# Gated delta rule in chunks of 64: block-diagonal chunk matrices, kept whole or as their blocks

## The chip, the core and the metric

The kernel runs on one core of a Trainium2 chip. TensorE (PE in the profile) multiplies, VectorE (DVE), ScalarE (ACT) and GpSimd (POOL) work on the elements, SyncE (SP) issues the DMA transfers. The metric is the device time of one execution in microseconds (us); lower is better. All data are fp32.

## The reference, cut to what matters

The program is two models in a row: two layers of a hybrid transformer block, then a second block whose token mixer is a gated delta rule, run forward and backward in time, followed by a mixture of 16 experts. The change touches the delta rule only: 4 heads of width 128, two directions, a context of 256 tokens (states alone, no queries) and then 512 tokens with queries, in chunks of 64.

```python
idx = jnp.arange(CHUNK)                                   # CHUNK = 64
incl = idx[:, None] >= idx[None, :]
decay = jnp.where(incl, jnp.exp(jnp.minimum(g[..., :, None] - g[..., None, :], 0.0)), 0.0)
m = jnp.where(idx[:, None] > idx[None, :], jnp.einsum('bhnik,bhnjk->bhnij', k_beta, kc) * decay, 0.0)
p = -m
t_inv = eye + p
for _ in range(CHUNK.bit_length() - 2):                   # five times
    p = p @ p
    t_inv = t_inv @ (eye + p)
w_blk = jnp.einsum('bhnij,bhnjk->bhnik', t_inv, k_beta * jnp.exp(g)[..., None])
u_blk = jnp.einsum('bhnij,bhnjv->bhniv', t_inv, vc * bc)
def advance(s, w_n, u_n, kt_n, sd_n):                     # once per chunk, in order
    u_new = u_n - jnp.einsum('bhik,bhkv->bhiv', w_n, s)
    return s * sd_n + jnp.einsum('bhik,bhiv->bhkv', kt_n, u_new), u_new
# with queries: o_n = q_dec @ s + (q k^T * decay) @ u_new
```

## The kernel before

Each engine has a program of its own, written out by hand in order, and the engines meet at counting semaphores. In the delta stage the class `Delta` (lines 499 to 522) counts named events: `says("KK", ins)` marks an instruction as the event KK of its engine, `needs("dve", "LT")` waits for an event of another. The order of each engine's list is the order of its code: PE lines 1189 to 1280, ACT 1736 to 1760, POOL 1885 to 1931, DVE 2298 to 2364.

The stage runs NT = 6 steps. A step takes a tile of 128 tokens (two chunks of 64) for each direction, and 4 heads for each direction, which are 8 units (U8; the first four are "f", the last four "b"). Steps 0 and 1 are context (no queries), steps 2 to 5 have queries (`x` is true). Each unit's chunk matrix is stored as 128 by 128 with two diagonal blocks of 64 by 64 that matter; the masks `tri` and `strict` make the rest zero. `pair(i)` is a pair of PSUM banks that holds 8 such matrices; there are four pairs.

The parts of a step, by event:
- Head. DVE TRILA (line 2315) spreads the log decays; PE G (1218) sums them with a matrix of ones, and KK, QK (1222, 1224) multiply keys by keys and keys by queries; PE KTOK and VTOK (1226, 1230) turn keys and values. DVE SUB and MIN (2319, 2321) and ACT E, EG (1746, 1748) make the decay matrix and the decay of the queries. POOL ETS and ETI (1903) mask it. DVE LT and QKD (2324, 2328) multiply it into KK and QK. PE L turns the result, DVE PM (2330) scales it by minus beta, PE PT turns it back, ACT PT (1754) copies that out.
- Rounds. Five doubling rounds on PE (1239 to 1253): SQ squares p, SQT squares its transpose (four rounds), TT multiplies it into the inverse; each for f and then b. ACT copies SQ out (1758), DVE copies SQT and adds TT (2337, 2340). Through the helper `each` (1206) all run as one matmul of 128 by 128 per unit.
- Tail. PE WT and U (1256, 1257), then for each of the two chunks WS, with queries Y (1273), and SU; at the end, with queries, X (1280). DVE U0f and so on (2350) subtract, S0f and so on (2355) update the state ST8, Y0 and X0 and so on (2362, 2364) add to the output. POOL scales keys, values and states (1914).

A matmul of the code is two passes through the array in the trace (fp32), each with its weight load; a transpose is one.

After the stage come a head norm, the output projection, the router, and the experts (PE line 1362), whose weights SP loads (line 716) once PE has signalled that the output projection is over (line 1305).

Of the kernel before, what the change touches and what calls it, by code (L numbers as in the profile page):

```python
# [99 lines left out]
K_TRI, K_STRICT = N_FIRST, N_FIRST + 2 * P  # L100
K_SAME = K_STRICT + 2 * P
# [7 lines left out]
def shape_constants():  # L109
# [9 lines left out]
    before = i[:, None] <= i[None, :]  # L119
    for d, m in enumerate((before, before.T)):  # L120
        c[:, K_TRI + d * P:K_TRI + (d + 1) * P] = m & same
        c[:, K_STRICT + d * P:K_STRICT + (d + 1) * P] = m & same & (i[:, None] != i[None, :])
# [27 lines left out]
def build(nc, A, out, debug=None):  # L150
    with ExitStack() as ctx:
# [192 lines left out]
        tri = c2[:, 0:2 * P].rearrange("p (d n) -> p d n", d=2)  # L344
        strict = c2[:, K_STRICT - K_TRI:K_STRICT - K_TRI + 2 * P].rearrange("p (d n) -> p d n", d=2)
# [20 lines left out]
        tail_half = take(NT * U8, 2)  # L366
# [26 lines left out]
        PTA, PTB, TT, ST8 = [view(i * U8 * P, U8, P, of=zf) for i in range(4)]  # L393
# [40 lines left out]
        def pair(i):  # L434

            return banks[:, 2 * i:2 * i + 2, :].rearrange("p b (h n) -> p (b h) n", n=P)

# [46 lines left out]
        def events(step):  # L484
# [3 lines left out]
                "pe": ["G", "KK"] + x * ["QK"] + ["KTOK", "VTOK", "L", "PT"]  # L488
# [3 lines left out]
                "dve": ["TRILA", "SUB", "MIN", "LT"] + x * ["QKD"] + ["PM", "TT0"]  # L492
                + [f"{n}{r}{d}" for r in r5 for n in (("SQT", "TT") if r < 5 else ("TT",)) for d in "fb"]
                + ["U"] + [f"{n}{c}{d}" for c in (0, 1) for n in ("U", "S") for d in "fb"] + x * ["Y0", "X0", "Y1", "X1"],
                "act": ["E"] + x * ["EG"] + ["KTOK", "VTOK", "PT"] + [f"SQ{r}{d}" for r in r5 for d in "fb"] + ["WT"],
                "pool": ["ETS", "ETI"] + x * ["QD"] + ["KBG", "KT0", "KT1", "VB", "SD0", "SD1"],
# [228 lines left out]
        def _(pe):  # L725
# [447 lines left out]
            for d in range(2):  # L1173
                pe.matmul(gs[:, :, d * DH:(d + 1) * DH], tri[:, d, :], la[:, :, d * DH:(d + 1) * DH], start=True, stop=True)
# [14 lines left out]
            for step in range(NT):  # L1189
# [16 lines left out]
                def each(i, lhsT, rhs, turn=False, units=slice(0, U8)):  # L1206
                    for un in range(U8)[units]:
                        o = pair(i)[:, un, :]
                        mm = pe.transpose(o, lhsT(un), ident) if turn else \
                            pe.matmul(o, lhsT(un), rhs(un), start=True, stop=True)  # L1210
                    return mm


                needs("dve", "TRILA")
                if step == 0:
                    pe.wait_ge(l2_ok, 2 * DH)
                for d in range(2):
                    mm = pe.matmul(ps[d][:, :], ones, E[:, d * DH:(d + 1) * DH, :].rearrange("p u n -> p (u n)"),
                                   start=True, stop=True)
                says("G", mm)  # L1220
                key = lambda un: kT[:, un % DH, cols(un)]
                says("KK", each(1, key, key))
                if x:
                    says("QK", each(2, key, lambda un: qT[:, un % DH, xcols(un)]))

                says("KTOK", each(3, key, None, True))
                needs("dve", "SUB")
                if x:
                    needs("act", "EG")
                says("VTOK", each(0, lambda un: vT[:, un % DH, cols(un)], None, True))  # L1230

                needs("dve", "LT")
                says("L", each(1, lambda un: ETS[:, un, :], None, True))
                needs("dve", "PM")
                says("PT", each(2, lambda un: PA[:, un, :], None, True))
# [3 lines left out]
                for r in range(1, 6):  # L1239
                    p0, pt0, p1 = Ps[(r - 1) % 2], PTs[(r - 1) % 2], Ps[r % 2]  # L1240
                    for d, units in DIRS.items():
                        if r == 1:
                            needs("act", "VTOK")
                        else:
                            needs("dve", f"SQT{r - 1}{d}")
                        says(f"SQ{r}{d}", each(3, lambda un: pt0[:, un, :], lambda un: p0[:, un, :], units=units))
                    if r < 5:
                        for d, units in DIRS.items():
                            says(f"SQT{r}{d}", each(0, lambda un: p0[:, un, :], lambda un: pt0[:, un, :], units=units))
                    for d, units in DIRS.items():  # L1250
                        needs("act", f"SQ{r}{d}")
                        needs("dve", f"TT{r - 1}{d}" if r > 1 else "TT0")
                        says(f"TT{r}{d}", each(1 if r % 2 else 2, lambda un: p1[:, un, :], lambda un: TT[:, un, :], units=units))
                needs("dve", "TT5b")
                needs("pool", "VB")
                says("WT", each(3, lambda un: KBG[:, un, :], lambda un: TT[:, un, :]))
                says("U", each(0, lambda un: TT[:, un, :], lambda un: VB[:, un, :]))
                needs("act", "WT")

                for c in range(2):  # L1260
                    for d, units in DIRS.items():
# [6 lines left out]
                        says(f"WS{c}{d}", each(1, lambda un: PTB[:, un, :], lambda un: ST8[:, un, :], units=units))  # L1268
                    if x:
                        for un in range(U8):  # L1270
                            h = c if un < DH else 1 - c
                            part = slice(h * CHUNK, (h + 1) * CHUNK)
                            mm = pe.matmul(pair(3)[:, un, part], ST8[:, un, :], EG[:, un, part], start=True, stop=True)
                        says(f"Y{c}", mm)
# [1199 lines left out]
```

## Time and profile before

| what | value |
|---|---|
| median of 3 runs | 3387.52 us (3384.53 to 3387.95) |
| the profiled execution, its own time | 3385.13 us |
| its span in the profile | 3382.6 us |
| PE busy / DVE / ACT / POOL | 86% / 35% / 22% / 7% of the span |
| delta stage in the trace | 2261 us to 2636.4 us: 375 us, 11% of the span |
| granted TensorE clock, mean | 0.94 |

The profile gives for each engine when each instruction began and how long it took, and what ended the idle time before it. PE is the matmul side of TensorE, PEld its weight loads. The chain is the path of work that ended last, followed back from the end: what is on it sets the time. PEclk is the share of full clock that was granted: 1.00 is 2.4 GHz, and a value between 0.5 and 1 is a mixture of that and 1.2 GHz over the stretch.

### The profile page before, as it was taken

Reading aid. Unit: us, or ns where it says so; the run is one execution under the profiler, and the core shown is the slowest. Engines: PE = TensorE matmul, PEld = TensorE weight load, DVE = VectorE, ACT = ScalarE, POOL = GpSimd, SP = SyncE. Lnnn points to the kernel's source line nnn. Section 1 sums busy time; section 2 is a strip of 40 time slices with the busy share of each in tenths; the row PEclk is TensorE's granted clock in tenths of the full one; section 3 lists DMA queues with packets and bytes.
Section 4 is the critical chain, followed back from the end, with each engine's and each line's share of the span. In section 5 each row is a group of like instructions: output and inputs, shape, how many; then the busy total and the mean of one; then the engine's idle time right before and its main releaser. Section 6 shows DMA issues by size and latency. Waiting matters only on the chain.

```text
span 3382.6 us, 31088 instructions
## 1 busy us (share of the span) xinstructions
PE 2896.7 (86%) x11890; PEld 1825.1 (54%) x11890; DVE 1170.3 (35%) x1663; ACT 751.2 (22%) x1169; POOL 241.1 (7%) x156
## 2 busy tenths in 40 slices
PE   7978888899989798788999959978888758777778
PEld 3324566688854235565888834648788444222223
DVE  0176234433330392544333334364444340000001
ACT  2133232322221242332212131141111022000001
POOL 0120000000000300000000006012332010000000
PEclk9989999999999899999999989889989869999999
DMA  4123211224230132211333231000000026999990
GB/s 143 50 75 120 80 50 57 68 81 113 84 113 22 50 136 88 75 50 50 87 94 100 81 109 44 32 25 1 1 1 1 0 87 275 410 409 410 409 381 25
DMA packets 256104, 379.57 MB, mean 112 GB/s; under 512 B 9153, under 2 KB 170078, under 8 KB 255838
## 3 DMA queue, kind: packets, MB, share of 16 engines
q1 hardware_dynamic: 255966, 377.72, 31.3%
q8 instruction: 88, 1.44, 0.2%
q14 instruction: 50, 0.41, 0.0%
HBM read 375.59 MB, written 2.10 MB: 112 GB/s over the span
## 4 chain that ended last, share of the span: by engine, by line
PE 66%; DMA 13%; DVE 12%; ACT 4%; issue 3%; POOL 1%; SPq 0%; DVEq 0%; ACTq 0%; POOLq 0%; PEldq 0%
PE banks L790 29%; PE banks L766 11%; PE banks L1093 9%; DMA ring<-in_w_up 8%; PE banks L1210 7%; DMA arena<-in_w_down 4%; DVE arena L2080 4%; PE banks L1362 2%; PE banks L776 1%; PE banks L782 1%; PE banks L1025 1%; PE banks L1340 1%; DVE stat L2061 1%; PE banks L1111 1%; DVE arena L2261 1%
## 5 line engine op out<-in xcount | busy, mean ns | idle before, releaser
L1549 ACT ACTIVATE w_hi<-ring 128x2048 fp32r<-128x2048 f32 (+1 forms) x100 | 174.4, 1746 | 544.2 <-PE banks L790 544.2
L790 PE MATMUL banks<-ffn_x_hi,w_hi 128*128 128x512 f32 x704 | 277.7, 394 | 16.7 <-DVE ffn_x_lo L1999 16.6
L790 PE MATMUL banks<-ffn_x_lo,w_hi 128*128 128x512 f32 x704 | 275.6, 391 | 0.0
L790 PE MATMUL banks<-ffn_x_hi,w_lo 128*128 128x512 f32 x704 | 275.4, 391 | 0.0
L1985 DVE TENSOR_TENSOR w_lo<-ring,w_hi 128x2048 fp32r<-128x2048 f32 (+1 forms) x100 | 207.5, 2077 | 78.8 <-ACT w_hi L1549 77.4
L1362 PE MATMUL banks<-ring,std 128*64 128x512 f32 x640 | 153.6, 603 | 46.3 <-DMA ring<-in_w_up 26.5
L766 PE MATMUL banks<-xT,ring 128*128 128x512 f32 (+1 forms) x416 | 183.5, 604 | 1.2 <-ACT taps L1453 1.2
L2080 DVE SCALAR_TENSOR_TENSOR arena<-arena,taps 128x512 f32<-128x512 f32 x240 | 163.3, 743 | 0.0
L790 PEld LDWEIGHTS banks<-ffn_x_hi,w_hi 128*128 128x128 f32 x704 | 132.9, 189 | 51.5 <-issue 17.9
L2449 DVE TENSOR_TENSOR gates<-gates,banks 128x512 f32<-128x512 f32 x16 | 11.0, 688 | 423.9 <-PE banks L1362 423.9
L1093 PE MATMUL banks<-zT,ring 128*128 128x512 f32 x320 | 144.7, 610 | 7.7 <-issue 6.9
L790 PEld LDWEIGHTS banks<-ffn_x_hi,w_lo 128*128 128x128 f32 x704 | 133.2, 189 | 28.0
L790 PEld LDWEIGHTS banks<-ffn_x_lo,w_hi 128*128 128x128 f32 x704 | 133.3, 189 | 26.6
L1210 PE MATMUL banks<-zT,arena 128*128 128x128 f32 x1152 | 141.9, 281 | 5.2 <-DVE zT L2340 4.7
L1210 PEld LDWEIGHTS banks<-zT,arena 128*128 128x128 f32 x1152 | 136.4, 197 | 6.9 <-DVE zT L2340 5.8
L790 PE MATMUL banks<-ffn_hidden_hi,w_hi 128*128 128x512 f32 x352 | 136.9, 389 | 0.0
L790 PE MATMUL banks<-ffn_hidden_lo,w_hi 128*128 128x512 f32 x352 | 136.9, 389 | 0.0
L790 PE MATMUL banks<-ffn_hidden_hi,w_lo 128*128 128x512 f32 x352 | 136.9, 389 | 0.0
L766 PEld LDWEIGHTS banks<-xT,ring 128*128 128x128 f32 (+1 forms) x416 | 79.7, 192 | 104.1 <-issue 104.1
L2182 DVE TENSOR_TENSOR squares<-gates,banks 128x512 f32<-128x512 f32 x44 | 30.2, 687 | 293.6 <-PE banks L790 293.6
L1362 PEld LDWEIGHTS banks<-ring,std 128*64 128x64 f32 x640 | 40.1, 136 | 158.7 <-DMA ring<-in_w_up 64.4
L766 PE MATMUL banks<-arena,ring 128*128 128x256 f32 (+2 forms) x384 | 115.7, 463 | 9.6 <-DVE arena L2036 9.6
(363 smaller groups left out, 4493.6 us busy)
## 6 DMA issues: line engine op xcount, KB each, us to landing
ring<-in_w_up SPq DMA_DIRECT2D x48, 1024.0 KB, 18.4
arena<-in_w_down SPq DMA_DIRECT2D x48, 1024.0 KB, 18.4
ring<-in_ffn_w_in SPq DMA_DIRECT2D x88, 512.0 KB, 4.5
ring<-in_w_gate SPq DMA_DIRECT2D x32, 1024.0 KB, 18.0
ring<-in_w_mod SPq DMA_DIRECT2D x24, 1024.0 KB, 7.2
ring<-in_xa_w_kv SPq DMA_DIRECT2D x16, 1024.0 KB, 6.2
zT<-in_w_gate SPq DMA_DIRECT2D x16, 1024.0 KB, 18.5
zT<-in_w_up SPq DMA_DIRECT2D x16, 1024.0 KB, 18.4
```

Source lines behind the costliest of these rows:

```text
L766: mm = pe.matmul(bank[0:m, 0:width], weights(k), rhs(k), start=(k == 0), stop=(k == n - 1))
L776: mm = pe.matmul(ps[bank][:, :], ones, zT[:, t, :], start=(t == 0), stop=(t == KT - 1))
L782: mm = pe.matmul(ps[bank + 1][:, :], ones, squares[:, t % 2, :], start=(t == 0), stop=(t == KT - 1))
L790: mm = pe.matmul(bank[:, :], weights(wp, k), rhs(rp, k), start=(k == 0 and wp == rp), stop=(k == n - 1 and wp == 1))
L1025: mm = pe.matmul(ps[4 + v][:, :], xv[:, kt, h * XD + v * P:h * XD + (v + 1) * P], probsT[:, kt, :], start=(kt == 0), stop=(kt == MT - 1))
L1093: mm = pe.matmul(out, weights(k), rhs(k), start=(k == 0), stop=(k == n - 1))
L1111: mm = pe.matmul(ps[1 + m % 2][:, 0:n], ones, squares[:, t % 2, 0:n], start=(t == 0), stop=(t == KT - 1))
L1210: pe.matmul(o, lhsT(un), rhs(un), start=True, stop=True)
L1362: mm = pe.matmul(bank[n * CAP:(n + 1) * CAP, :], tokens, weights[:, n * 512:(n + 1) * 512], start=first, stop=last)
L1549: nc.scalar.activation(w_split[n % 2][0][:, 0:m], raw[n % 2][:, 0:m], ACT.Copy).then_inc(f_hi.sem, 1)
L1985: V.tensor_tensor(lo[:, 0:m], raw[n % 2][:, 0:m], hi[:, 0:m].bitcast(F32), ALU.subtract).then_inc(f_lo.sem, 1)
L2080: V.scalar_tensor_tensor(out=acc, in0=x, scalar=c, in1=acc, op0=ALU.mult, op1=ALU.add)\
```

## The change

The chunk matrices keep only their diagonal blocks: a unit's matrix becomes 128 rows by 64 columns (rows 0 to 63 hold the first chunk's block, rows 64 to 127 the second's), so tiles of 8 x 128 columns become 8 x 64. The helper `small` multiplies each unit in two matmuls of 64 by 64 by 64, one on the array's upper left quarter and one on its lower right. Masks are applied by DVE as KKM and QKM straight from PSUM; POOL's ETS and ETI go, and POOL makes the product QKD. The decay of the queries gets matmuls of its own (GX) into pair 3, where KTOK comes next and waits for EG. The keys' tail scaling needs one POOL product (KT) where it took two (KT0, KT1), since SU reads only the rows of its chunk. KK and QK move ahead of G, and wait for the last step's last addition (X1 or S1b). L and PT become products with a block of the identity. WT, U, SU and X contract over 64 rows, WS has 64 columns of weights. The small set-up step `tail_half` goes.

```diff
-        E, ETS, ETI, EG, KBG, KT0, KT1, VB, PA, PB = [take(U8, P) for _ in range(10)]
+        E, GD, ETS, ETI, PA, PB, PTA, PTB, TT = [take(U8, CHUNK) for _ in range(9)]
+        KBG, KD, VB = [take(U8, P) for _ in range(3)]
+        EG = take(2, U8, CHUNK)
+        def blocks(i):
+            return banks[:, 2 * i:2 * i + 2, 0:DH * CHUNK].rearrange("p b (h n) -> p b h n", n=CHUNK)
+        def by_chunk(i):
+            return banks[:, 2 * i:2 * i + 2, :].rearrange("p c (u n) -> p c u n", n=CHUNK)
...
-                needs("dve", "TRILA")
-                for d in range(2):
-                    mm = pe.matmul(ps[d][:, :], ones, E[:, d * DH:(d + 1) * DH, :].rearrange("p u n -> p (u n)"),
-                                   start=True, stop=True)
-                says("G", mm)
-                key = lambda un: kT[:, un % DH, cols(un)]
-                says("KK", each(1, key, key))
+                def small(i, lhsT, rhs, units=slice(0, U8)):
+                    for un in range(U8)[units]:
+                        for c, rows in enumerate(CHUNKS):
+                            mm = pe.matmul(blocks(i)[rows, un // DH, un % DH, :], lhsT(un, rows), rhs(un, rows),
+                                           start=True, stop=True)
+                    return mm
+                if step == 0:
+                    pe.wait_ge(l2_ok, 2 * DH)
+                else:
+                    needs("dve", "X1" if step - 1 >= CTX // P else "S1b", step - 1)
+                says("KK", small(1, key, key))
+                if x:
+                    says("QK", small(2, key, lambda un, rows: qT[:, un % DH, xtokens(un, rows)]))
+                needs("dve", "TRILA")
+                for d in range(2):
+                    for rows in CHUNKS:
+                        mm = pe.matmul(blocks(0)[rows, d], ones[rows, 0:CHUNK], E[rows, d * DH:(d + 1) * DH, :],
+                                       start=True, stop=True)
+                says("G", mm)
+                if x:
+                    for c, rows in enumerate(CHUNKS):
+                        mm = pe.matmul(by_chunk(3)[:, c], ones[rows, :], E[rows, :, :], start=True, stop=True)
+                    says("GX", mm)
+                    needs("act", "EG")
+                says("KTOK", transposed(3, lambda un: kT[:, un % DH, cols(un)]))
...
-                        says(f"SQ{r}{d}", each(3, lambda un: pt0[:, un, :], lambda un: p0[:, un, :], units=units))
+                        says(f"SQ{r}{d}", small(3, lambda un, rows: pt0[rows, un, :], lambda un, rows: p0[rows, un, :], units))
...
-                says("WT", each(3, lambda un: KBG[:, un, :], lambda un: TT[:, un, :]))
-                says("U", each(0, lambda un: TT[:, un, :], lambda un: VB[:, un, :]))
+                        mm = pe.matmul(by_chunk(3)[:, c, un, :], KBG[rows, un, :], TT[rows, un, :], start=True, stop=True)
+                        mm = pe.matmul(pair(0)[rows, un, :], TT[rows, un, :], VB[rows, un, :], start=True, stop=True)
...
+                            mm = pe.matmul(pair(1)[CHUNKS[half_no], un, :], WT[:, half_no, un, :], ST8[:, un, :],
+                                           start=True, stop=True)
+                            mm = pe.matmul(pair(2)[:, un, :], KD[rows, un, :], VN[rows, un, :], start=True, stop=True)
+                            mm = pe.matmul(by_chunk(1)[:, c, un, :], VN[rows, un, :], ETI[rows, un, :], start=True, stop=True)
...
-                for name, dst, m in (("ETS", ETS, strict), ("ETI", ETI, tri)):
-                    for d in range(2):
-                        ins = G.tensor_tensor(dst[:, r, :], E[:, r, :], masked(m)[d], ALU.mult)
+                    says("QKD", G.tensor_tensor(ETI, ETI, E, ALU.mult))
-                says("KT0", scaled(KT0, KT1, th[:, :, 0]))
-                says("KT1", scaled(KT1, KT1, th[:, :, 1]))
+                says("KT", scaled(KD, KD, tail[:, step, :]))
...
-                    ins = V.tensor_tensor(E[:, r, :], tri[:, d:d + 1, :].broadcast_to([P, DH, P]),
-                                          la[:, step, r].unsqueeze(2).broadcast_to([P, DH, P]), ALU.mult)
-                says("TRILA", ins)
+                says("TRILA", V.tensor_tensor(by_dir(E), each_dir(tri), each_col(la[:, step, :]), ALU.mult))
+                says("KKM", V.tensor_tensor(by_dir(ETS), blocks(1), each_dir(strict), ALU.mult))
+                    says("QKM", V.tensor_tensor(by_dir(ETI), blocks(2), each_dir(tri), ALU.mult))
+                says("SUB", V.tensor_tensor(by_dir(GD), blocks(0), each_col(gsum[:, step, :]), ALU.subtract))
+                says("LT", V.tensor_tensor(ETS, ETS, E, ALU.mult))
```

## Rows read from the trace of the kernel before


**Rows 1.** The page: span, and granted clock in 40 equal slices of it.
```profile
span 3382.6 us, 31088 instructions
...
PEclk9989999999999899999999989889989869999999
```

**Rows 2.** Windows by step: length; busy PE, PEld, DVE, ACT, POOL; PEclk, DMA, GB/s.
```profile
2261.00:2317.00 56.00, 47.82 (x372) 45.10 (x372) 25.21 (x33) 10.98 (x16) 17.16 (x10) 0.91 0.00 1
2317.00:2374.00 57.00, 48.19 (x372) 45.47 (x372) 26.41 (x35) 10.90 (x15) 17.16 (x10) 0.91 0.00 1
2374.00:2439.50 65.50, 55.40 (x436) 52.00 (x436) 30.12 (x40) 11.94 (x16) 19.51 (x12) 0.92 0.00 1
2439.50:2506.10 66.60, 56.53 (x436) 53.41 (x436) 30.09 (x40) 11.94 (x16) 19.51 (x12) 0.90 0.00 1
2506.10:2571.20 65.10, 55.73 (x436) 53.05 (x436) 31.07 (x41) 11.93 (x16) 19.51 (x12) 0.92 0.00 1
2571.20:2636.40 65.20, 55.64 (x436) 52.64 (x436) 30.84 (x39) 11.94 (x16) 19.51 (x12) 0.92 0.00 1
```

**Rows 3.** The chain through step 3: start, length, what.
```profile
2439.45 1.21 DVE arena L2315 x2
...
2440.71 3.38 PE banks L1218 x4
...
2447.24 4.98 POOL arena L1903 x4
...
2456.73 1.03 ACT zT L1754
...
2457.81 28.30 PE banks L1210 x224
...
2486.13 0.70 DVE zT L2340
...
2486.87 5.62 PE banks L1210 x48
2492.49 1.73 PE banks L1273 x16
```

**Rows 4.** The chain through step 1, context only.
```profile
2333.05 27.57 PE banks L1210 x224
...
2361.39 3.85 PE banks L1210 x32
```

**Rows 5.** Timeline inside the rounds: start, length, instruction, idle before and releaser.
```profile
2471.57 1.95 PE L1210 MATMUL banks<-arena,zT 128*128 128x128 f32 x16
2472.67 0.60 ACT L1758 ACTIVATE arena<-banks 128x512 f32<-128x512 f32 x1 [3.87 <-PE banks L1210]
2473.36 3.74 PE L1210 MATMUL banks<-zT,arena 128*128 128x128 f32 x32
```

**Rows 6.** Timelines: a 128-column stream, then the experts' 64-column one and its loads.
```profile
2097.09 7.03 PE L1093 MATMUL banks<-zT,ring 128*128 128x512 f32 x16
...
2902.41 1.94 PE L1362 MATMUL banks<-ring,std 128*64 128x512 f32 x8 [0.62 <-DMA ring<-in_w_gate]
...
2902.41 0.20 PEld L1362 LDWEIGHTS banks<-ring,std 128*64 128x64 f32 x4 [1.50 <-DMA ring<-in_w_gate]
```

**Rows 7.** Two weight loads by line: ns least, median, most.
```profile
L1362 PEld LDWEIGHTS banks<-ring,std x640: 132/137/137, 2817.6 to 3285.0; 128*64 128x64 f32 x160
...
L1210 PEld LDWEIGHTS banks<-zT,arena x1152: 186/192/333, 2279.8 to 2631.4; 128*128 128x128 f32 x192
```

**Rows 8.** A window of the expert stage (columns as in Rows 2, clock third from the end).
```profile
2900.00:3000.00 100.00, 76.55 (x326) 21.04 (x326) 3.16 (x6) 8.42 (x13) 0.00 (x0) 1.00 1.03 409
```

**Rows 9.** Groups by form: count, busy us, mean ns, idle before.
```profile
L2265 DVE TENSOR_TENSOR arena<-arena 128x256 f32<-128x256 f32 x4 | 1.7, 419 | 0.0
...
L1668 ACT ACTIVATE arena<-banks 128x256 f32<-128x256 f32 x8 | 3.1, 385 | 68.9 <-PE banks L1093 68.9
```

**Rows 10.** Waits of SP's own queue.
```profile
SPq L716 <- PEq L1305: 518.2, 1, 518.2
```

More of the change, by code:

```diff
@@ L118, in shape_constants @@
         c[NOPE + j, K_SWAP + NOPE + h + j] = 1.0
[L119 to L122, printed above, removed]
+    row, col = i[:, None] % CHUNK, i[None, :CHUNK]
+    for d, m in enumerate((row <= col, row >= col)):
+        c[:, K_TRI + d * CHUNK:K_TRI + (d + 1) * CHUNK] = m
+        c[:, K_STRICT + d * CHUNK:K_STRICT + (d + 1) * CHUNK] = m & (row != col)
+    c[:, K_EYE:K_EYE + CHUNK] = row == col
     c[:, K_SAME:K_SAME + P] = same
@@ L1204, in xcols, with transposed @@
                     return slice(t * P, (t + 1) * P)
-                def each(i, lhsT, rhs, turn=False, units=slice(0, U8)):
+                def transposed(i, src):
+                    for un in range(U8):
+                        mm = pe.transpose(pair(i)[:, un, :], src(un), ident)
+                    return mm
+                def small(i, lhsT, rhs, units=slice(0, U8)):
                     for un in range(U8)[units]:
-                        o = pair(i)[:, un, :]
-                        mm = pe.transpose(o, lhsT(un), ident) if turn else \
-                            pe.matmul(o, lhsT(un), rhs(un), start=True, stop=True)
-                    return mm
@@ L1234, in _ @@
+                says("L", small(1, lambda un, rows: ETS[rows, un, :], same_block))
                 needs("dve", "PM")
-                says("PT", each(2, lambda un: PA[:, un, :], None, True))
+                says("PT", small(2, lambda un, rows: PA[rows, un, :], same_block))
                 needs("act", "PT")
@@ L1753, in _ @@
                 needs("pe", "PT")
-                says("PT", A1(PTA, pair(2), ACT.Copy))
+                says("PT", A1(by_dir(PTA), blocks(2), ACT.Copy))
                 for r in range(1, 6):
@@ L2317, in _ @@
-                says("TRILA", ins)
-                needs("pe", "G")
-                says("SUB", V.tensor_tensor(E, pair(0), every(gsum[:, step, :]), ALU.subtract))
-                needs("dve", "SUB")
-                says("MIN", V.tensor_scalar(E, E, 0.0, None, ALU.min))
+                if step and step - 1 >= CTX // P:
+                    needs("pool", "QKD", step - 1)
+                says("TRILA", V.tensor_tensor(by_dir(E), each_dir(tri), each_col(la[:, step, :]), ALU.mult))
                 needs("pe", "KK")
-                needs("pool", "ETS")
@@ L2329, in _ @@
+                needs("dve", "SUB")
+                says("MIN", V.tensor_scalar(GD, GD, 0.0, None, ALU.min))
+                needs("act", "E")
+                needs("dve", "KKM")
+                says("LT", V.tensor_tensor(ETS, ETS, E, ALU.mult))
                 needs("pe", "L")
-                says("PM", V.tensor_tensor(PA, pair(1), every(nbeta[:, step, :]), ALU.mult))
+                says("PM", V.tensor_tensor(by_dir(PA), blocks(1), each_col(nbeta[:, step, :]), ALU.mult))
                 needs("act", "PT")
-                says("TT0", V.tensor_tensor(TT, PTA, ident.unsqueeze(1).broadcast_to([P, U8, P]), ALU.add))
+                says("TT0", V.tensor_tensor(TT, PTA, eye.unsqueeze(1).broadcast_to([P, U8, CHUNK]), ALU.add))
```

152 lines of the change are left out of this document (83 added, 69 removed).

## The prediction

> **What bounds the kernel now.** I read the page first for the span and the clock [rows 1], then windows for the time of each step of the delta stage [rows 2], then the chain through a step with queries [rows 3] and through one without [rows 4], and last the timeline inside the doubling rounds [rows 5]. The six steps take 56.0, 57.0, 65.5, 66.6, 65.1 and 65.2 us, 375.4 in all, one behind the other [rows 2]. In step 3 the chain has three stretches: a head of 18.4 us (2439.45 to 2457.81), in which each engine waits for another and POOL's masking alone takes 4.98; rounds of 29.1 (to 2486.87), in which PE is the chain for 28.3; and a tail of 19.3, mostly PE again [rows 3]. So PE's passes in the rounds and the hand-overs in the head are what a change can shorten. Behind the stage nothing catches up: SP's queue stands at the expert weights for 518.2 us until PE reports the output projection [rows 10], so the DMA-fed experts start earlier by whatever the delta stage gives up. I take it one for one.
>
> **The unit of the sum: a pass.** A group of 4 units, 8 passes with weights of 128 columns, takes 0.895 us: 16 passes start at 2471.57 and the next ones at 2473.36, and ACT starts on the first half 1.10 after its first pass, 0.20 behind its last slot [rows 5]. So a pass costs 0.112 and a hand-over 0.20 (0.05 from ACT or DVE to PE, as from 2439.45 + 1.21 to 2440.71 in [rows 3]). Halving the moving columns alone brings nothing: line 1273 moves 64 columns with weights of 128, and its 16 passes take 1.73, 0.108 each [rows 3]. What holds it is the weight load. Loads last 192 ns for 128 columns and 137 for 64 [rows 7], 55 ns for each 64 columns, so a pass of 64 by 64 should hold its part of the array for about 0.055 to 0.058. I take 0.058, a load in the same proportion above its 0.055 as 0.112 above the 0.108.
>
> The change needs twice the passes (two quarters per unit), so all hangs on whether quarters overlap. The experts' 64-column matmuls go to two halves of the array in turn: 8 passes of 512 columns take 1.94, while 16 such passes with 128 columns take 7.03 [rows 6]. Taken off the last pass's tail (about 0.2), that is 0.43 for two passes against 0.43 for one: they overlap fully, in fp32. Four loads of 0.14 lie within 0.20 there [rows 6], so the fourth starts at most 0.06 behind the first, and the array takes loads for both halves within one slot. I therefore price a pair of quarters at 0.058, 0.029 for a pass. No row shows two *row* parts overlapping; the bounds are full overlap and none, and I take overlap since the halves are the nearest row.
>
> **Head with queries**, from the last addition of the step before: KK 16 pairs, 0.05 to 0.98; QK to 1.91; G, 8 passes of 256 columns in 4 pairs of 0.215 (half of 0.43), to 2.77, with TRILA (0.69) long done; a change of tile shape, which I bound by nothing and one hand-over, at 0.2; GX, 4 passes of 512 in 2 pairs, to 3.83; hand-over; EG on ACT (1.03 for 1024 columns, as the copy in [rows 3]) to 5.06. That is a new wait: KTOK stands behind EG on PE, and VTOK, L and the rest behind KTOK. KTOK and VTOK, 16 single passes, end at 6.9. Beside them: DVE's KKM, QKM, SUB and MIN (0.70 each for 512 columns) end before 5, E on ACT (0.60 [rows 5]) follows EG to 5.7, LT ends at 6.4, so it is hidden. L with a shape change 7.1 to 8.03; PM to 8.93; PT to 9.90; ACT's copy to 10.7; the rounds start at 10.8. That is 7.6 less than 18.4. POOL's QD, QKD, KBG, KT and VB, some 10 us, lie under the rounds.
>
> **Head without queries**: no QK, GX or EG. G ends at 1.84, SUB, MIN (0.69 as the bound), E and LT end at 4.85 and are now what ends last, since VTOK is over at 3.8. Rounds start at 8.6 against 16.3 in step 1 (window start 2316.7 to 2333.05 [rows 2, 4]): 7.7 less.
>
> **Rounds.** A group of 4 units is 8 pairs, 0.464. In rounds 1 to 4 PE has six groups, 2.78. Is something else late? DVE takes 0.42 for 256 columns and ACT 0.39 [rows 9]: an SQT starts at 0.93, is copied by 2.02, needed at 2.78; DVE works 1.7 of 2.78. So PE stays the bound: 11.1. Round 5 is latency: SQ 0.46, hand-over, ACT 0.39, then TT, 2.0 in all; then DVE 0.42 with its hand-overs, 0.7. Sum 13.8, against 29.1 in step 3 and 28.3 in step 1 (2333.05 to 2361.39): 15.3 and 14.5 less.
>
> **Tail.** WT, U and X have twice the passes, but 128 columns of weights or of moving data keep each at 0.112, so as pairs they cost what they did (32 passes in pairs, 1.8). WS, Y and SU have as many passes as before and go group by group. DVE's and ACT's pieces there keep their sizes. I add 0.7 a step for three or four unhidden shape changes, and 1.0 for passes at the lower clock: the steps have a clock of 0.90 to 0.92 [rows 2] with head gaps above 1 us, and such gaps remain. Both are bounded below by nothing; above, 1.7 could be 4.
>
> **Sum.** Step 3 gains 7.6 + 15.3 - 1.7 = 21.2; the mean of the four steps with queries is 65.6 against 66.6, because of clock I no longer expect, so 20.2, times 4 is 80.8. Steps 0 and 1 gain 7.7 + 14.5 - 1.7 less 0.5 (mean 56.5 against 57.0) = 20.0 each, 40.0. The set-up step and the four small matmuls that replace two cancel within 0.5. The profiled execution took 3385.1, so 3385.1 - 120.8 = 3264.3; the median of the runs lies 2.4 above it: **3267 us**.
>
> **Rivals.**
> - *No overlap of quarters* (the change doesn't do what it says; ends slower). The stage issues 3392 passes of the small kind (576 in a step with queries, 544 without) and 512 in WT, U and X. One by one they cost 3392 x 0.029 = 98 and 512 x 0.056 = 29 more, G and GX 9 more: 3403. It decides from 89% of the overlap lost. Against it: the halves in [rows 6]. For it: no row has two row parts. A milder form is a rule that two row parts may not write one PSUM bank at a time: both quarters of a `small` write one bank, as do those of U and G, while WT, X and GX write two. Then 98 + 11 + 5 are lost: 3381, within 0.2% of before. The Trainium skill states it ("TensorEngine Tiling (Array Packing)", Restrictions and Gotchas): different row tiles cannot access the same PSUM bank simultaneously. The trace only has two column halves in one bank, which overlap.
> - *Row parts overlap only where their columns differ too.* WT, X and GX go one by one: 320 x 0.056 + 3.4 = 21 more, 3288.
> - *The instruction stream.* Quarters want a load and a pass every 0.029. The densest long stream of the trace has one every 0.112 [rows 5]; only a burst of four loads [rows 6] is denser. If the queue runs dry, each 0.01 a pass costs 34 us; gain and loss meet at 0.063, and at 0.112 the time would be 3577. The Trainium skill ("TensorE: Matmul & The Clock Gate", Part 1) gives about 62 ns for each matmul when hardware decoding is off; by that figure, an estimate, the sum would be near 3382, no change. No run here shows which decoding is on.
> - *The clock.* If a stage of small tiles were held at 1.2 GHz, passes double: 98 for the small ones and 99 for the rest, 3464. Against it: half-width weights run at a clock of 1.00 [rows 8].
>
> **From cases to numbers.** The forecast (3240 to 3290): 0.62. Row parts in one column range not overlapping (3288): 0.12. A stream somewhat slower than 0.029, up to 0.053 (3290 to 3350): 0.08, and up to 3381: 0.03. Bank rule, or a pace near the 0.063 where gain and loss meet: 0.07. Slower: no overlap 0.03, pace over 0.063 0.03, clock 0.02. A measurement of this kernel tells about 0.2% (7 us) from no change. So faster 0.85, same 0.07, slower 0.08. The range's low end is a slot of 0.055 and PE running WS and SU of the two directions beside one another, since they now sit in different parts of the array (up to 0.9 x 4 a step, 21 us): 3240. Its high end takes in the rows case and a stream of 0.05: 3345.
>
> **What would show it.** After: rounds of some 14 us in each step; six groups in 2.8; PE starts two by two; a window of a step with queries of about 45 us and of one without about 37; POOL gone from the chain; ACT's EG in the chain ahead of KTOK. Wrong if the small passes start 0.05 or more apart without a wait, or if the clock row of the stage falls below 0.8. The same gain must appear as an earlier start of the expert stage, whose length stays.

## The result, and the profile of the kernel after

The kernel after takes 3263.2 us (median of 4 runs, 3260.07 to 3264.21), against 3387.52 before: the ratio is 0.963, with a 95% interval of 0.962 to 0.9648, so 124 us less. The forecast was 3267, with a range of 3240 to 3345. The profiled execution took 3262.29 us; its span is 3260.5.

The page of the kernel after, its span and the granted clock in 40 slices, which answer to [rows 1]:

```profile
span 3260.5 us, 35240 instructions
...
PEclk9989999999999989999999997998999869999999
```

The same windows as in [rows 2], one for each step of the delta stage (length; busy PE, PEld, DVE, ACT, POOL; granted clock, DMA share, GB/s):

```profile
2262.50:2297.60 35.10, 30.57 (x696) 28.12 (x696) 18.40 (x34) 7.91 (x15) 9.86 (x5) 1.00 0.01 3
2297.60:2332.70 35.10, 30.57 (x696) 28.12 (x696) 18.95 (x35) 7.91 (x15) 9.85 (x5) 1.00 0.01 3
2332.70:2376.70 44.00, 37.81 (x796) 34.61 (x796) 22.87 (x40) 8.93 (x16) 13.87 (x8) 0.99 0.01 2
2376.70:2422.00 45.30, 39.06 (x796) 35.86 (x796) 22.92 (x40) 8.93 (x16) 13.87 (x8) 0.95 0.01 3
2422.00:2468.40 46.40, 40.22 (x796) 36.45 (x796) 22.86 (x40) 8.93 (x16) 13.86 (x8) 0.94 0.01 2
2468.40:2513.90 45.50, 39.26 (x796) 36.06 (x796) 22.89 (x39) 8.93 (x16) 13.88 (x8) 0.95 0.01 2
```

The stage takes 251.4 us where it took 375.4, so 124.0 of the time saved is here, and the two spans differ by 122.1. Each step has nearly twice the passes (796 against 436) in two thirds of the time, and its clock is higher (0.94 to 1.00 against 0.90 to 0.92). Behind the stage nothing catches up: the last 480.5 us of both kernels are the same work at the same pace. The first row below is that window after, the second the same window before; POOL is idle in both and the DMA share is 0.84 in both:

```profile
2780.00:3260.50 480.50, 371.32 (x1460) 116.11 (x1460) 27.52 (x42) 51.31 (x81) 0.00 (x0) 0.99 0.84 337
```

```profile
2902.00:3382.50 480.50, 371.35 (x1460) 116.15 (x1460) 27.51 (x42) 51.37 (x81) 0.00 (x0) 0.99 0.84 337
```

The wait of SP's queue that was 518.2 us [rows 10] is now this one, in the list of waits (engine, line, what it waits for: us in all, times, longest):

```profile
SPq L747 <- PEq L1377: 393.8, 1, 393.8
```

It is 124.4 shorter, as much as the stage gave up. The chain through step 3 (start, length, what), where [rows 3] had POOL's masks and passes of line 1210; KK and QK are the first row, G and GX the next two, then EG on ACT:

```profile
2376.74 3.33 PE banks L1249 x64
2380.07 1.01 PE banks L1273 x8
2381.08 1.08 PE banks L1278 x4
...
2382.19 1.03 ACT arena L1819
...
2383.26 1.97 PE banks L1241 x16
2385.23 1.11 PE banks L1249 x32
...
2388.30 0.61 ACT arena L1827
...
2388.95 12.35 PE banks L1249 x416
...
2401.32 1.17 PE banks L1249 x32
...
2402.51 0.43 DVE arena L2395
...
2402.99 2.00 PE banks L1312 x32
2404.99 1.89 PE banks L1318 x32
2406.89 1.51 PE banks L1332 x16
2408.40 1.93 PE banks L1338 x16
```

The reader is to see three things. First, the rounds are 14.0 us (2388.95 to 2402.94), where they were 29.1: 416 passes in 12.35, 0.0297 each. Second, POOL is gone from the chain; KTOK and VTOK (line 1241) begin 0.04 behind EG. Third, the head is 12.2 us and no longer a chain of three engines' turns only: its largest piece is KK and QK, 64 passes in 3.33, or 0.052 each, nearly twice what a pass costs in the rounds.

The timeline inside the rounds, as in [rows 5] (idle time before, and what ended it, in brackets):

```profile
2392.02 0.42 DVE L2395 TENSOR_TENSOR arena<-arena,banks 128x256 f32<-128x256 f32 x1
2392.21 3.38 PE L1249 MATMUL banks<-arena 64*64 64x64 f32 x110
...
2392.48 0.85 ACT L1831 ACTIVATE arena<-banks 128x256 f32<-128x256 f32 x2 [1.95 <-PE banks L1249]
2393.42 0.89 DVE L2392 COPY arena<-banks 128x256 f32<-128x256 f32 x2 [0.98 <-PE banks L1249]
...
2394.35 0.89 DVE L2395 TENSOR_TENSOR arena<-arena,banks 128x256 f32<-128x256 f32 x2
2395.28 0.38 ACT L1831 ACTIVATE arena<-banks 128x256 f32<-128x256 f32 x1 [1.95 <-PE banks L1249]
```

A round lasts 2.80 us (ACT starts at 2392.48 and 2395.28); DVE works 1.78 of it, ACT 0.85, and PE has no gap. The single starts in the trace come in pairs: of the intervals between starts of the 3392 passes of line 1249, 1617 are 6 or 7 ns and 1398 are 51 or 52 ns. So two quarters start together, and the next two follow 0.052 behind. One thing said of the change needs setting right: KK and QK contract over all 128 rows (the trace has them as 128*64), so their two passes are column halves of the array; quarters are G, L, PT, U and the products of the rounds. The starts of KK and QK in step 2 come in pairs just as well.

### The profile page after: what moved, and what is told of

It reads as the page before. It is cut to its first block, busy times and chain, and to the rows that moved or that the text cites. A ratio compares the mean times of both kernels' runs of the same rounds, so it can differ in the third digit from the quotient of the medians.

```text
span 3260.5 us, 35240 instructions
## 1 busy us (share of the span) xinstructions
PE 2797.1 (86%) x13982; PEld 1725.3 (53%) x13982; DVE 1124.2 (34%) x1656; ACT 733.2 (22%) x1169; POOL 203.9 (6%) x130
## 4 chain that ended last, share of the span: by engine, by line
PE 66%; DMA 14%; DVE 12%; ACT 4%; issue 3%; POOL 1%; SPq 0%; DVEq 0%; ACTq 0%; POOLq 0%; PEldq 0%
PE banks L821 30%; PE banks L797 11%; PE banks L1124 9%; DMA ring<-in_w_up 8%; DMA arena<-in_w_down 5%; DVE arena L2145 4%; PE banks L1249 3%; PE banks L1434 2%; PE banks L807 1%; PE banks L813 1%; PE banks L1056 1%; PE banks L1412 1%; DVE stat L2126 1%; PE banks L1142 1%; DVE arena L2326 1%
## 5 line engine op out<-in xcount | busy, mean ns | idle before, releaser
L821 PE MATMUL banks<-ffn_x_hi,w_hi 128*128 128x512 f32 x704 | 277.7, 394 | 16.4 <-DVE ffn_x_lo L2064 16.3
L1249 PE MATMUL banks<-arena 64*64 64x64 f32 (+1 forms) x3008 | 95.9, 224 | 15.1 <-DVE arena L2419 8.5
L1124 PEld LDWEIGHTS banks<-zT,ring 128*128 128x128 f32 x320 | 62.1, 195 | 82.1 <-issue 81.5
```

The lines of the kernel that those rows point to most:

```text
L821: mm = pe.matmul(bank[:, :], weights(wp, k), rhs(rp, k), start=(k == 0 and wp == rp), stop=(k == n - 1 and wp == 1))
L1124: mm = pe.matmul(out, weights(k), rhs(k), start=(k == 0), stop=(k == n - 1))
L1249: mm = pe.matmul(blocks(i)[rows, un // DH, un % DH, :], lhsT(un, rows), rhs(un, rows), start=True, stop=True)
```

## The experiments

Theory A is the prediction's: a pass on a quarter is paced by its weight load, the two quarters overlap, PE is the bound of the rounds, and the heads gain by the moved masks. Its rivals: quarters don't need each other (B in the first run), the stream of instructions or the copies set the pace, the moved columns set it, and the gain in the head is from elsewhere. Each run is compared with 3263.2 us, the kernel after, or with 3387.5, the kernel before; a ratio is always to the kernel before, run again beside it (medians of 3385.3 to 3386.6). A difference below some 7 us is told as what it is, not as a finding.

**1. The same passes, quarter by quarter.** All passes of one quarter of a group go first (8 where a group is one direction, 16 where it is both), then all of the other:

```diff
-                    for un in range(U8)[units]:
-                        for c, rows in enumerate(CHUNKS):
+                    for c, rows in enumerate(CHUNKS):
+                        for un in range(U8)[units]:
```

> After's kernel, with one line order changed: a group issues all its passes for the upper left quarter first and then all for the lower right, 8 and 8, where they took turns. Same passes, same waits. Theory A (quarters overlap because the next instructions in TensorE's queue go to the other quarter; it looks past a few waiting ones only): each pass then costs about 0.058 us alone, so 3392 x 0.029 = 98 us more at most, some 70 to 98 us over after (3333 to 3361). Rival B (the queue reaches past 16 instructions, or overlap is not what made the rounds short): no change, 3263.

Measured: 3311.4 us (3310.14 to 3313.84), ratio 0.9778 [0.9762, 0.9795], 48 more than after. Two pieces of its chain in step 2 (L, then the rounds), and the windows of the rounds in steps 1 and 2:

```profile
2358.62 1.85 PE banks L1249 x32
...
2363.82 16.79 PE banks L1249 x448
```

```profile
2317.90:2337.10 19.20, 19.16 (x448) 18.99 (x448) 8.89 (x18) 3.84 (x10) 1.16 (x1) 0.85 0.01 3
2363.80:2380.60 16.80, 16.77 (x448) 16.60 (x448) 8.62 (x18) 3.84 (x10) 5.04 (x3) 1.00 0.01 4
```

Where 16 passes of one quarter precede 16 of the other, 32 passes take 1.85, and the single starts in the trace lie 58 or 59 ns apart: this is the price of an unpaired pass that the prediction took. Only where the quarter changes are there three pairs of starts 4 or 5 ns apart. The rounds, with 8 and 8, show the same three pairs at a change, each time: of 8 starts 3 come 4 to 6 ns behind another, which leaves 5 slots of 58 ns, and a pass costs 0.037 at a clock of 1.00 (16.79 / 448). Theory A had not foreseen this part of the overlap, so the run falls below its 3333 to 3361. In five of the six steps the rounds also take 19.2 to 19.4 at a clock of 0.83 to 0.85. So the gain does rest on the order of the quarters; the 48 us are of two kinds, the lost overlap (3.3 us in the rounds of each step and 0.7 for each of KK, QK, L and PT, some 35 in all) and the lower clock (some 2.5 in the rounds of five steps, some 12 in all).

**2. Two and two.** To see how far ahead a pass may begin, the quarters change after two passes:

```diff
+                    some = list(range(U8)[units])
+                    for two in (some[k:k + 2] for k in range(0, len(some), 2)):
                         for c, rows in enumerate(CHUNKS):
-                            mm = pe.matmul(...)
+                            for un in two:
+                                mm = pe.matmul(...)
```

> The kernel after, with the quarters taken in turn by two units instead of one: two passes on the upper left quarter, then two on the lower right. Theory A: passes may begin ahead of an earlier one that still waits for its own quarter, over a reach of a few passes (the runs of eight in q1_order still ran at 0.037 a pass at full clock), so two and two overlap fully: 3262 to 3268 us, rounds 13.5 to 14. Rival B: only the very next pass can begin beside the one that runs; then of each four passes one pair overlaps and the pace is 0.043 a pass, 3392 x 0.014 = 49 us more, near 3310.

Measured: 3265.5 us (3262.8 to 3268.97), ratio 0.9646 [0.963, 0.9662]. The rounds in step 2 and in step 1:

```profile
2347.00:2359.40 12.40, 12.39 (x416) 12.26 (x416) 7.61 (x17) 3.46 (x9) 6.23 (x4) 1.00 0.02 4
...
2307.10:2321.70 14.60, 14.60 (x416) 14.50 (x416) 8.92 (x17) 3.46 (x9) 3.91 (x2) 0.83 0.01 3
```

The first is what the kernel after has (12.35), so alternation needn't be strict: runs of two overlap fully, and longer runs overlap for three passes at each change of quarter. The second row is step 1, 2.2 us longer at a clock of 0.83; the other five steps have 12.39 or 12.40. Whether the order brings that about isn't shown: in experiment 8 the rounds of step 4, with strict alternation, take 14.66 at 0.82.

**3. Twice the stream.** Each small product issued twice, with nothing else changed:

```diff
+                        for n in (64, CHUNK):
-                        for c, rows in enumerate(CHUNKS):
+                            for c, rows in enumerate(CHUNKS):
```

> After's kernel, but each small matmul is issued twice into the same place (the pair first, then the pair again), so 3392 passes more. Theory A (PE is what bounds the rounds, and a pair of passes costs 0.058): 3392 x 0.029 = 98 more, 3361. Rival B (rounds are held by the hand-overs to ScalarE and VectorE, so that passes have slack): clearly less, under 50 more.

Measured: 3358.6 us (3356.11 to 3362.03), ratio 0.9915 [0.9898, 0.9931], 95 more than after for 3392 more passes: 0.028 each. The rounds:

```profile
2325.91 26.37 PE banks L1250 x896
```

Theory A's price holds (26.37 / 896 = 0.0294), also over a stream that lasts 26 us without a gap. This also answers the rival of the instruction stream: a load and a pass every 0.029 us is sustained, an instruction each 15 ns, and the queue does not run dry.

**4. Fewer columns moved.** The same, where the extra pass moves 16 columns (q3_thin) or 32 (q4_half) of the 64:

```diff
-                        for n in (64, CHUNK):
+                        for n in (16, CHUNK):
```

> As q2_twice, but the first of the two issues moves 16 columns instead of 64; weights are loaded in full (64 columns). Theory A (the weight load sets the 0.058 of a pair): as much as q2_twice, 3361. Rival B (the moving columns set it): a quarter of it, some 25 more, 3288.

> The kernel after, with each small product issued twice as in q2_twice, where the first of the two moves 32 of the 64 columns. Theory A: a pass of a quarter is paced by its weight load and not by the columns that it moves, so the time is that of q2_twice, 3358 us, and each five rounds take 26.4 us with the clock at 1.00. Rival B: the columns set the pace, then the rounds are shorter by a quarter, about 20 us, near 3325. Rival C: what kept the clock at 0.50 in four steps of q3_thin does it here too, then the rounds of those steps take 48 us and the time is above 3420.

With 32 columns: 3358.0 us (3356.73 to 3360.08), ratio 0.9921 [0.9905, 0.9938], the same as in 3. Every step's rounds take 26.37 at a clock of 1.00, one of them here:

```profile
2374.80:2401.20 26.40, 26.35 (x896) 26.21 (x896) 8.24 (x18) 3.84 (x10) 4.66 (x3) 1.00 0.02 4
```

So half the columns in half the passes change nothing: the load sets the pace. With 16 columns the runs lie between 3397.09 and 3484.3, median 3475.07, and no ratio is given, since the runs themselves differ by 87 us. Even the shortest is 39 above the run with 32 columns. The trace is of an execution of 3468.66 us. The windows of its rounds in steps 0, 2 and 3:

```profile
2276.30:2324.40 48.10, 48.05 (x896) 47.86 (x896) 8.35 (x18) 3.83 (x10) 0.63 (x1) 0.50 0.01 2
...
2406.90:2433.20 26.30, 26.30 (x896) 26.17 (x896) 8.16 (x18) 3.83 (x10) 4.60 (x3) 1.00 0.02 4
2473.40:2521.40 48.00, 48.00 (x896) 47.82 (x896) 8.80 (x18) 3.83 (x10) 3.37 (x2) 0.50 0.01 3
```

At a clock of 1.00 the rounds take 26.3, so there too the load sets the pace, as theory A said. But in four of six steps (0, 3, 4 and 5) the clock stays at 0.50 or 0.51, 1.2 GHz, through rounds in which PE has not one gap, and they take 47.7 to 48.1. Neither theory expected it. The run differs from the one with 32 columns in that number alone, so thin passes are what brings it about; four such steps are 86 of the 111 us by which this execution is above the run with 32 columns. Why the same stream is granted full clock in two steps and not in the others stays open. The prediction's rival of the clock is therefore real for thinner passes and does not touch the kernel's own, of 64 columns.

**5. The copies of the rounds twice.** ACT's copy of SQ and DVE's of SQT are made a second time, into a spare tile:

```diff
+                        A1(XA[:, r % 2][:, units, :], blocks(3)[:, "fb".index(d)], ACT.Copy)
                         says(f"SQ{r}{d}", A1((PA, PB)[r % 2][:, units, :], blocks(3)[:, "fb".index(d)], ACT.Copy))
...
+                            V.tensor_copy(XV[:, r % 2][:, units, :], blocks(0)[:, "fb".index(d)])
                             says(f"SQT{r}{d}", V.tensor_copy((PTA, PTB)[r % 2][:, units, :], blocks(0)[:, "fb".index(d)]))
```

> The kernel after, with each copy of SQ on ScalarE and of SQT on VectorE in the rounds done a second time into a spare tile first. Theory A: PE is the bound of the rounds and both engines have slack (VectorE 1.8 of 2.8 us, then 2.6 of 2.8), so only round 5, which is latency, shows it: 0.4 us a step and some slips, +2 to +8 us, 3266 to 3271. Rival B: the rounds hang on the copies: 8 more copies of 0.43 us on VectorE in each of six steps, +21 us, 3284.

Measured: 3265.0 us (3262.72 to 3267.73), ratio 0.9642 [0.9626, 0.9658]: 1.8 more, just under theory A's 2 to 8 and far from 21. The end of the rounds in step 2 is where it shows:

```profile
2346.11 11.91 PE banks L1250 x400
...
2358.43 0.28 ACT arena L1833
...
2358.75 1.26 PE banks L1250 x32
```

Only round 5 waits for ACT's second copy. From 2346.11 to the end of DVE's last addition at 2360.47 it is 14.36 against 14.0 in the kernel after, and six times 0.36 is 2.2. So PE alone bounds the rounds, with at least the 0.9 us of slack on DVE that the two extra copies of a round took up.

**6. The masks of the head, put back.** The kernel after, with its masks made by POOL as before, on the narrow tiles:

```diff
-                "dve": ["TRILA", "KKM"] + x * ["QKM"] + ["SUB", "MIN", "LT", "PM", "TT0"]
+                "dve": ["TRILA", "SUB", "MIN", "LT"] + x * ["QKD"] + ["PM", "TT0"]
...
+                for name, dst, m in (("ETS", ETS, strict), ("ETI", ETI, tri)):
+                    says(name, G.tensor_tensor(by_dir(dst), by_dir(E), each_dir(m), ALU.mult))
```

> After's kernel with the masks back on GpSimd (ETS and ETI made from the decay, at the new width of 64 columns), LT and QKD from PSUM on VectorE; all else is after's. Theory A (at half width GpSimd's masks cost little): L about 0.7 us later and PM 0.2 behind QKD with queries, LT 1.3 later without, so 4 x 0.9 + 2 x 1.3 = 6 more, 3269. Rival B (the mask order is worth as much as in the wide kernel): 15 more or over, 3278.

Measured: 3273.4 us (3272.14 to 3275.48), ratio 0.9668 [0.9653, 0.9682], 10 more. In the chain of a step with queries stand

```profile
2393.26 2.53 POOL arena L1971 x2
...
2395.88 0.69 DVE arena L2384
```

so the masks alone, half as wide, cost 2.53 on POOL, and it is part of the head again (13.1 us from KK to the rounds, against 12.2, the 0.9 that theory A gave a step). The rest of the 10 is mostly clock. The rounds of steps 0 and 1, 12.35 in the kernel after, take 14.00 and 14.53 here, 3.8 more for the same 416 passes, and this is step 1:

```profile
2312.60:2327.10 14.50, 14.50 (x416) 14.39 (x416) 7.94 (x17) 3.45 (x9) 2.94 (x2) 0.83 0.02 5
```

In the other four steps they are as in the kernel after. What is left of the 10 is the 6 that theory A gave; the 3.8 of clock it did not have.

**7. The masks of the head alone, on the kernel before.** DVE applies the masks to KK and QK as they leave PSUM, at the full width of 128, and POOL makes the product QKD; PE's passes stay as they are:

```diff
-                "pool": ["ETS", "ETI"] + x * ["QD"] + ["KBG", "KT0", "KT1", "VB", "SD0", "SD1"],
+                "pool": x * ["QKD", "QD"] + ["KBG", "KT0", "KT1", "VB", "SD0", "SD1"],
...
+                    ins = V.tensor_tensor(ETS[:, r, :], pair(1)[:, r, :], strict[:, d:d + 1, :].broadcast_to([P, DH, P]), ALU.mult)
+                says("KKM", ins)
```

> The kernel before with one part of the change alone: the masks go from GpSimd to VectorE (straight from PSUM, while ScalarE makes the decay), at full width, and GpSimd makes only the product QKD. Whole matrices, no quarters. Theory A (the order and GpSimd's masks are the smaller part of the gain, the width and the quarters the larger): from the end of MIN to PM 5.1 us in place of 7.3 with queries and 4.0 in place of 6.9 without, so 4 x 2.2 + 2 x 2.9 = 15 less than before, 3373. Rival B (GpSimd's 5 us on the chain are the head's whole gain): 25 to 35 less, 3353 to 3362.

Measured: 3363.0 us (3359.24 to 3365.05), ratio 0.9929 [0.9912, 0.9945], 24 less than before, between what the two theories gave. Its rounds in step 3, with the same 224 passes that took 28.30 in [rows 3]:

```profile
2443.30:2468.70 25.40, 25.34 (x224) 25.15 (x224) 14.69 (x19) 5.97 (x10) 10.32 (x6) 1.00 0.01 2
```

They are 2.9 shorter, at a clock of 1.00; in the kernel before the same stretch (2457.80 to 2486.10) has 0.89. This is the step with the largest difference. Over the six steps the 224 passes take 26.82, 27.57, 26.86, 28.30, 28.10 and 27.81 before, and 26.86, 25.35, 26.98, 25.35, 26.81 and 25.35 here: 8.8 less in all, and nothing in steps 0 and 2. The six heads, each from its step's start to its rounds, give 16.4 (from 103.0 to 86.6), near theory A's 15. So the gain is theory A's, and with it clock in the rounds that neither theory had.

**8. The order of the transposes.** In a step with queries VTOK, which doesn't use pair 3, goes ahead of KTOK, so that less waits for EG:

```diff
+                    says("VTOK", transposed(0, lambda un: vT[:, un % DH, cols(un)]))
                     needs("act", "EG")
                 says("KTOK", transposed(3, lambda un: kT[:, un % DH, cols(un)]))
```

> After's kernel, but in steps with queries PE turns the values (VTOK, which waits only for SUB) before the keys (KTOK, which waits for EG), so that only half of the turning stands behind the new wait. Theory A (in after's trace LT ends at 2385.11 and L starts at 2385.17, so LT was as late as the turning and is what comes next): within 1 us of 3263. Rival B (the wait for EG was the head's bound): 0.9 x 4 = 3.6 less, 3260.

Measured: 3261.3 us (3259.18 to 3262.46), ratio 0.963 [0.9617, 0.9643], 1.9 less, which can't be told from nothing. The medians alone can't choose between the two theories, which are 3.6 apart. The trace can: from KK to the rounds step 3 takes 12.16 against 12.21 in the kernel after. The transposes leave the chain, and LT takes their place.

```profile
2379.20 1.02 ACT arena L1822
2380.22 0.53 ACT arena L1824
...
2380.78 1.36 DVE arena L2385
```

**9. No idle stretch between the steps.** The head's largest piece is KK and QK at a low clock. Here PE is given work of the next step while DVE still adds the output: TRILA of the next step is made behind the last state update, the additions are ordered Y, Y, X, X, and PE's order is QK, G, GX, KK, each behind the one event that frees its bank:

```diff
-                "pe": ["KK"] + x * ["QK"] + ["G"] + x * ["GX"] + ["KTOK", "VTOK", "L", "PT"]
+                "pe": x * ["QK"] + ["G"] + x * ["GX"] + ["KK"] + ["KTOK", "VTOK", "L", "PT"]
...
-                + ["U"] + [f"{n}{c}{d}" for c in (0, 1) for n in ("VN", "S") for d in "fb"] + x * ["Y0", "X0", "Y1", "X1"],
+                + ["U"] + [f"{n}{c}{d}" for c in (0, 1) for n in ("VN", "S") for d in "fb"]
+                + (step < NT - 1) * ["NEXT"] + x * ["Y0", "Y1", "X0", "X1"],
```

> After's kernel with the head of a step pulled under the tail of the one before: TRILA of the next step right behind S1b, the additions in the order Y0, Y1, X0, X1, the Y ones before X has ended, and on PE QK, G, GX before KK, so that only KK waits for the last addition. Same instructions. Theory A (in steps behind one with queries PE stands idle for 2.8 us before KK and then runs KK and QK at half clock, 3.3 us in place of 2.1): L comes 4 to 6 us earlier in steps 3 to 5 and 1 to 2 in steps 1 and 2, in all 14 to 20 less, 3243 to 3249, and the clock of steps 3 to 5 goes from 0.95 to near 1. Rival B (VectorE's queue is the head's bound, the additions and six products in a row): under 8 less, 3255 or more.

Measured: 3243.6 us (3241.11 to 3243.85), ratio 0.9578 [0.9565, 0.9591]: 20 less than after, faster than both kernels. Its step 3 begins right behind X, the first row (chain, then the window of the step):

```profile
2371.32 1.73 PE banks L1360 x31
2373.05 1.08 PE banks L1250 x32
2374.13 1.01 PE banks L1276 x8
2375.14 1.06 PE banks L1283 x4
2376.20 1.08 PE banks L1250 x32
```

```profile
2373.00:2413.20 40.20, 37.90 (x799) 34.70 (x798) 22.15 (x40) 8.94 (x16) 13.88 (x8) 1.00 0.01 3
```

QK and KK take 1.08 each, 2.16 together against 3.33, and the step 40.2 us at a clock of 1.00 against 45.3 at 0.95. PE is busy for 37.9 of the 40.2. Of the 5.1 us, 2.8 are the idle time between the steps, 1.2 the clock of KK and QK, and 1.1 the wait for EG, which KK now covers. Step 1 doesn't gain as theory A had it: from the rounds of step 0 to its own it takes 36.5 us against 35.1, with G at 1.92 and KK at 1.82 at the lower clock.

## Why the prediction was right

**The pass and its overlap.** The pair of quarters was priced at 0.058, a pass at 0.029; the rounds give 0.0297, and the extra passes of experiment 3 cost 0.028. The load of 64 columns takes 135 ns in the trace, as the 137 of [rows 7]. The unpaired 0.058 stands in experiment 1, in the starts 58 or 59 ns apart. The choice of the column halves in [rows 6] as nearest row for row parts was right.

**Rounds.** 13.8 was said and 14.0 came in all six steps; six groups take 2.80 where 2.78 was said. DVE is not late, and experiment 5 bounds its slack.

**Head without queries.** 8.6 was said, and step 1 has 8.6 (2297.63 to 2306.22).

**Head with queries.** 10.8 was said; steps 2 to 5 have 11.0, 12.2, 13.4 and 12.4. This is the term that was mis-sized. KK and QK were priced at 1.86. They take 2.09 in step 2, where little idle time stands before them, and 3.33, 3.68 and 3.54 in steps 3 to 5, where PE has stood idle while DVE adds the outputs, for 2.84 us in step 3, and the first passes behind that run at the lower clock. This is the window of the first 2.76 us of KK and QK in step 3, with the clock third from the end:

```profile
2376.74:2379.50 2.76, 2.76 (x52) 2.76 (x54) 1.23 (x2) 0.00 (x0) 0.00 (x0) 0.50 0.02 6
```

The trace of before had shown this: G's 4 passes of 512 columns take 3.38 in [rows 3], 0.85 each, twice the 0.43 of [rows 6], behind the same additions. I put this into one allowance of 1.0 a step, at the tail, and not into the first term of the head. Experiment 9 takes that idle time away, and the pieces take 1.08 each.

LT took 1.35, and not the 0.70 that the same line takes in step 1, while POOL ran its product of QD beside it (2383.29 to 2386.24), and ended at 2385.11, 0.06 before L. The prediction had it end 0.5 before the transposes; it is hidden with next to nothing to spare, and experiment 8 shows it as what is late next.

**Tail.** 19.3 + 1.7 was said for step 3, and 19.0 came (2402.99 to 2421.97). The shape changes cost nothing that can be seen: in the chain one piece follows the other within 0.01. WS of both directions takes 1.51 for 16 passes, so they run in part beside one another, the effect that the range's low end had at up to 0.9 for each of four places; it gives some 0.2 at a step's first WS. The two errors, +1.4 in the head and -2.0 in the tail, nearly cancel: the step was forecast at 45.6 and took 45.3. In steps 0 and 1 only the tail's part is there, and they take 35.1 where 36.5 was said, which is most of the 4 us by which the forecast was too high.

**The whole stage.** The prediction's terms give the six heads 46 us, the six rounds 90, and the tails 10 more time than before; it then took off 5 for clock. The traces give the heads 37 (from 103 to 66), the rounds 86 (from 170 to 84) and the tails 1. The rounds are a forecast that held; that the total came within 4 us is in part luck, since the heads fell 9 short and the rounds 4, and the tails and the allowance for clock were 16 too cautious.

**The rivals.** No overlap (3403) falls with the pairs of starts, and experiment 1 shows what a lost overlap costs. The rule that two row parts may not write one bank at a time (3381), from the Trainium skill, "TensorEngine Tiling (Array Packing)", Restrictions and Gotchas, is not borne out here. Both quarters of a unit in the rounds, in G and in U write one bank, on different partitions; 32 passes of U take 1.89, and those of WT, which write two banks, 2.00. Even by that rule KK and QK, being column halves, would have lost nothing, and the sum would have been 3372. Row parts in the same columns (3288) overlap as well: WT, X and GX are such, and WT's 32 passes start in pairs, 0.0625 each over the piece, where one by one they would take 0.112 each. The stream of instructions is no bound at 0.029 for a load and a pass, nor in experiment 3. The 62 ns of the Trainium skill ("TensorE: Matmul & The Clock Gate", Part 1) for a matmul without hardware decoding, which would have given 3382, are not seen here. The clock held down (3464) did not happen with passes of 64 columns, and did, in four steps of six, with every other one of 16.

**What was assumed without a reason.** The forecast knew that the steps had a clock of 0.90 to 0.92, and took its rounds at full clock. In the kernel after that came true: the rounds have 1.00 in all six steps (the window 2388.9 to 2403.0 is step 3). But it was not safe. In the kernel before, the six rounds together are 13 us longer than six times the 25.35 that they take at 1.00 in experiment 7, and the moved masks alone give back 8.8 of that. Narrow kernels lose clock in the rounds too: in experiment 6 in steps 0 and 1, in experiment 2 in step 1, and in experiment 8 in step 4, behind a head of 13.7 us where the kernel after has 13.4. Each has one trace, and what decides in which step the rounds lose clock isn't settled. So of the 86 us that the rounds gave, some 73 are narrower matrices in quarters, and 13 clock that the kernel before had lost. How much of the 37 in the heads is the masks' isn't a plain share either: moving them is worth 24 in all on the kernel before and 10 on the kernel after, in both cases with some clock in it.

## What to carry to other kernels

Where fp32 passes are paced by their weight load, block-diagonal operands should be cut into quarters of the array and issued in turn: two quarters run in the time of one, and the order of issue is what decides it, with runs of two as good as strict alternation, and longer runs losing more the longer they are. When PE becomes the bound of a stage, look next at its longest idle stretch and at what it does right after: here it stood still for 2.8 us, then ran its first passes at 1.2 GHz, and giving it the next step's products while another engine finishes the last one brought 20 us more. Read the clock of every step before calling a difference the edit's: single steps gained or lost 2 us of rounds by it. Don't thin the passes of a long stream to a few columns without looking at the clock row.

## What the runs showed of the hardware that was not expected

- Two quarters start 6 or 7 ns apart and the next two 51 or 52 ns later; 0.029 us for a load and a pass is held over 26 us.
- Passes start ahead of earlier ones that wait for their own quarter, since with runs of two on each quarter all are paired (0.030 a pass); but only so far: with runs of 8 and of 16 there are three pairs at each change of quarter, and 58 ns between the other starts (0.037 a pass in runs of 8).
- With every other pass moving 16 columns, the clock stays at 0.50 or 0.51 through rounds of 48 us in four of six steps; with 32 columns it is 1.00 in the rounds of all six.
- DVE's product of 512 columns takes 1.35 us while POOL's product runs, and 0.70 in step 1, where POOL makes no such product (line 2383 in both). PM (line 2385), of the same size but with one input in PSUM, takes 0.69 in all six steps, in step 2 with POOL's products beside it (2338.01 to 2342.19). That POOL causes it is argued from the time alone.
- With POOL's masks gone from the heads of the kernel before, the rounds of four of six steps are 1.3 to 2.9 us shorter for the same passes; in step 3, the largest, the clock goes from 0.89 to 1.00.
